# A two-block fp32 kernel on one core: TensorE multiplies a constant identity first, and the first k-tile's passes are put in another order

## The reference

```python
def hybrid_layer(x, norm_g, w_in, b_forget, pool_w, pool_scale, w_up_pool, w_up_attn, w_out):
    h = rmsnorm(x, norm_g)                        # 528 tokens (16 meta + 512) x 1024
    proj = jnp.einsum('bld,dn->bln', h, w_in)     # w_in: 1024 x 5128
    u_pool, z_pool, q, k, v, z_attn, f_logit, g_pool, g_attn = jnp.split(proj, _split_points(), axis=-1)
...
def reference(...):
    x = first_block(x, meta_tokens, norm_g, w_in, b_forget, pool_w, pool_scale, w_up_pool, w_up_attn, w_out,
                    final_norm_g)
    return second_block(x, c_2, g_norm1_2, w_in_2, g_q_2, g_k_2, rel_bias_2, w_o_2, g_norm2_2, w1_2, w2_2,
                        w_ada_2, b_ada_2)
```

## Time and profile before

| | |
|---|---|
| time, median of 3 runs | 1047.46 us (1045.13 to 1049.05) |
| the profiled execution's own time | 1048.44 us |
| its span, first to last instruction | 1046.4 us |
| TensorE matmuls busy | 992.7 us (95%) |
| TensorE weight loads busy | 817.5 us (78%) |
| VectorE busy | 675.7 us (65%) |
| ScalarE busy | 488.3 us (47%) |
| GpSimd busy | 86.1 us (8%) |
| mean granted TensorE clock | 0.988 |

### The profile page before, as it was taken

The page is one execution under the profiler, slowest core; times in us unless marked ns, Lnnn a source line. Parts: engine busy times, 40 slices in busy tenths (PEclk is TensorE's granted clock), DMA queues, the critical chain, the costliest instruction groups (busy, mean ns, idle before and its releaser), DMA issues.

```text
span 1046.4 us, 13120 instructions
## 1 busy us (share of the span) xinstructions
PE 992.7 (95%) x4760; PEld 817.5 (78%) x4760; DVE 675.7 (65%) x1270; ACT 488.3 (47%) x977; POOL 86.1 (8%) x195
## 2 busy tenths in 40 slices
PE   6998998999999999999998978889999999999998
PEld 4887887878888888766777756788878888888886
DVE  6386776785888759367678885778354445444453
ACT  6256776563232346477886764334224323412420
POOL 0000000110122011000003332001000000000000
PEclk9999999999999999998999998999999999999999
DMA  8133233128887523433213221525732322331211
GB/s 296 60 102 111 83 102 89 45 65 339 300 304 281 198 114 148 105 109 99 91 48 115 61 61 66 215 81 129 133 112 90 121 81 81 121 121 57 105 61 60
DMA packets 29535, 129.82 MB, mean 124 GB/s; under 512 B 3864, under 2 KB 3864, under 8 KB 19872
## 3 DMA queue, kind: packets, MB, share of 16 engines
q1 hardware_dynamic: 19984, 98.27, 29.0%
q0 software_dynamic: 7472, 26.75, 7.2%
q10 hardware_dynamic: 2016, 3.97, 1.1%
HBM read 118.40 MB, written 4.22 MB: 117 GB/s over the span
## 4 chain that ended last, share of the span: by engine, by line
PE 71%; DVE 15%; issue 5%; ACT 4%; DMA 4%; POOL 1%; SPq 0%; ACTq 0%; POOLq 0%; DVEq 0%
PE psum L1730 22%; PE psum L1731 21%; PE psum L1732 21%; DVE sgt L1192 2%; DVE wl L994 2%; DVE ptl L1209 2%; PE psum L1861 2%; PE psum L1840 1%; PE psum L1881 1%; DMA k_sb<-k_sb 1%; PE psum L1883 1%; DVE p_sb L1200 1%; DVE two L1531 1%; DMA x1b<-x_kept 1%; PE psum L2112 1%
## 5 line engine op out<-in xcount | busy, mean ns | idle before, releaser
L1730 PE MATMUL psum<-hh,wh 128*128 128x512 f32 (+1 forms) x720 | 277.3, 385 | 0.0
L1731 PE MATMUL psum<-hl,wh 128*128 128x512 f32 (+1 forms) x720 | 268.4, 373 | 0.0
L1732 PE MATMUL psum<-hh,wl 128*128 128x512 f32 (+1 forms) x720 | 268.2, 373 | 0.0
L519 ACT ACTIVATE wh<-raw 128x512 fp32r<-128x512 f32 x292 | 169.4, 620 | 134.2 <-PE psum L1732 119.9
L994 DVE TENSOR_TENSOR wl<-raw,wh 128x512 fp32r<-128x512 f32 x292 | 192.4, 684 | 18.0 <-ACT wh L519 17.7
L1732 PEld LDWEIGHTS psum<-hh,wl 128*128 128x128 f32 x720 | 136.0, 189 | 23.8
L1730 PEld LDWEIGHTS psum<-hh,wh 128*128 128x128 f32 x720 | 136.2, 189 | 22.9 <-issue 3.0
L1731 PEld LDWEIGHTS psum<-hl,wh 128*128 128x128 f32 x720 | 136.3, 189 | 18.6 <-issue 0.5
L1730 PE MATMUL psum<-wh,ah 128*128 128x512 f32 x320 | 127.6, 399 | 5.7 <-DVE wl L994 3.4
L1732 PE MATMUL psum<-wh,al 128*128 128x512 f32 x320 | 126.0, 394 | 0.0
L1731 PE MATMUL psum<-wl,ah 128*128 128x512 f32 x320 | 126.0, 394 | 0.0
(11 more groups left out here) (247 smaller groups left out, 1512.0 us busy)
## 6 DMA issues: line engine op xcount, KB each, us to landing
raw<-in_wall SPq DMA_DIRECT2D x75, 1024.0 KB, 4.9
wa<-in_wada POOLq DMA_DIRECT2D x20, 512.0 KB, 5.6
gt<-in_wada POOLq DMA_DIRECT2D x20, 512.0 KB, 6.1
wb<-in_wada POOLq DMA_DIRECT2D x8, 512.0 KB, 6.0
xt<-in_xcols SPq DMA_DIRECT2D x8, 264.0 KB, 8.4
cb<-c_rows SPq DMA_DIRECT2D x8, 264.0 KB, 3.3
x<-in_x SPq DMA_DIRECT2D x4, 512.0 KB, 8.3
x_kept<-x SPq DMA_DIRECT2D x4, 512.0 KB, 2.8
```

Source lines behind the costliest of these rows:

```text
L519: e.activation(home(w)[0][:, 512 * c:512 * c + 512], raw_of(w, c), ACT.Copy).then_inc(a["wh"], 1)
L1730: e.matmul(out_, lh, rh, start=start, stop=False, skip_group_check=True)
L1731: e.matmul(out_, lh, rl, start=False, stop=False, skip_group_check=True)
L1732: return e.matmul(out_, ll, rh, start=False, stop=stop, skip_group_check=True)
```

## The change

Only PE's program changes. Ahead of everything it multiplies `ident` with `ident` twelve times into bank 6, after the wait for the constants; nothing reads the result, and bank 6 is written afresh later. Then k-tile 0 is written out: five passes hh·wh after waits on `act_wh` and `act_hh0`, then five passes hh·wl after `dve_wl`, then five passes hl·wh after `dve_hl0`. K-tiles 1 to 3 are as they were.

```diff
             e.wait_ge(g["const"], 8)
             cuts = [(META + 128 * i, 128, bank[i]) for i in range(4)] + [(0, META, bank[7][0:META, :])]
-            for k in range(4):
+
+            for _ in range(12):
+                e.matmul(bank[6][:, 0:128], ident[:, :], ident[:, :], start=True, stop=True)
+
+            e.wait_ge(a["wh"], 1)
+            e.wait_ge(a["hh0"], 1)
+            for c0, rows, bk in cuts:
+                e.matmul(bk, hh[:, 0, c0:c0 + rows], wh[:, 0, 0:512], start=True, stop=False,
+                         skip_group_check=True)
+            e.wait_ge(v["wl"], 1)
+            for c0, rows, bk in cuts:
+                e.matmul(bk, hh[:, 0, c0:c0 + rows], wl[:, 0, 0:512], start=False, stop=False,
+                         skip_group_check=True)
+            e.wait_ge(v["hl0"], 1)
+            for c0, rows, bk in cuts:
+                e.matmul(bk, hl[:, 0, c0:c0 + rows], wh[:, 0, 0:512], start=False, stop=False,
+                         skip_group_check=True)
+            for k in range(1, 4):
                 e.wait_ge(v["wl"], k + 1)
                 e.wait_ge(v["hl0"], k + 1)
                 for c0, rows, bk in cuts:
-                    ins = by_rows(0, k, k, bk, (hh, hl), c0, rows, k == 0, False)
+                    ins = by_rows(0, k, k, bk, (hh, hl), c0, rows, False, False)
             ins.then_inc(t["half"], 1)
```

## The result

The changed kernel takes 1040.16 us (median of 6 runs, 1036.23 to 1040.8), against 1047.03 us before (6 runs, 1045.13 to 1050.6). The ratio is 0.9923, 95% interval 0.9907 to 0.994: 0.77% faster. That is 6.9 us where 3.0 to 3.6 were forecast, and outside the range of 1041.2 to 1047.6.

The account below looks back on a forecast made before the run. TensorE, 71% of the chain, was taken as the bound, first waiting 8.5 us for hl. Identity work and reordered passes gain 3.6 us in the profiled execution, 3.0 typically: 1047.46 to 1044.4 us, range 1041.2 to 1047.6.

Parts of the forecast that it names:

- The identity's cost: At TensorE's start: 24 records at half clock, 0.23 us each, 5.5 us in all, ending at 7.97 us.
- the rise: At TensorE's start: identity work begun at 2.45 us brings full clock between 5.8 and 8.5 us.
- The second k-tile: K-tile 1 on TensorE starts at 11.3 us against 14.87, 3.6 us earlier, bounds 3.2 and 3.7.
- DVE's row at 28.00: DVE's first 128x4 row behind TensorE comes at 28.1 us where it was 31.70.
- The two new waits on DVE: In k-tile 0, the waits for wl and hl before the later pass groups hold nothing.
- the middle of executions: Whole kernel: with a clock rise midway between 3.3 and 6.1 us, the gain is 3.0 us.
- I find nothing that takes the 3.6 us back: After the start: later operands and loads don't hold TensorE, so the whole chain keeps the 3.6 us.
- the first step of the part by part: At TensorE's start: twelve identity matmuls make 24 records from 2.45 us, costing 5.5 us, upper bound 6.5.
- C: Rival, 0.20: later half-speed clock stretches come out otherwise; one more cancels the gain, one or two fewer double it.
- B: Rival, 0.15: the identity lifts the clock late or not at all at the start; gain 0.8 to 1.8 us.
- D: Rival, 0.05: the identity runs at weight-load speed without lifting the clock; k-tile 1 starts 1.7 us late, 1049.2 us.

Follow-up runs that it names:

- e3: The kernel before with only the twelve identity matmuls added, k-tile 0 in the old order: 1041.91 us, ratio 0.9944.
- e4: The kernel before with twelve tiny 16 x 2 matmuls on the identity ahead of everything, 48 added records with hardly any work: 1043.75 us, ratio 0.9968.
- e6: The kernel before, with POOL issuing the four wb loads only after the last of the four x1b reloads has landed: 1043.44 us, ratio 0.9964.
- e7: The changed kernel with POOL's wb loads held until the x1b reloads have landed: 1040.47 us, ratio 0.9935.
- e5: The kernel before with 64 tiny 16 x 2 matmuls on the identity ahead of everything, 256 added records: 1047.63 us, ratio 1.0009.
- e1: The kernel before, unchanged, run and traced once more: 1048.12 us, ratio 1.0008.
- e2: The changed kernel without the identity matmuls, leaving only the new pass order of the first k-tile: 1047.73 us, ratio 0.9993.
- e8: The changed kernel with 8 identity matmuls in place of 12: 1041.54 us, ratio 0.9955.

## Why the prediction was wrong

**The start, right.** The identity's cost was right: the first 16 of its records took 3.57 us at half clock (the 17th starts at 5.93), 0.22 each where 0.23 was forecast. It was hidden, ending before the tokens came, and it was followed by the clock at full; the rise fell at 6.15 (records 0.21 us apart before, 0.11 after), inside the forecast 5.8 to 8.5. The Trainium skill ("TensorE: Matmul & The Clock Gate", "Part 1: The HAM clock gate") has it that activity releases the throttle, and by that rule products of an identity should release it too; the traces agree, as e3 and the changed kernel ran nothing else before the tokens and began these at full speed. The second k-tile started at 11.19 (11.3 forecast), and DVE's row at 28.00 (28.1). The two new waits on DVE held nothing.

**What the start is worth in the time, about right.** Against e4, which has the fetch moved and the old start, the changed kernel's median is 3.6 us lower (1043.75 to 1040.16), but from other sets of runs; each against its own kernel before, it is 6.9 - 4.1 = 2.8. Against e6 on the same chip, e7 is 3.0 lower (1043.44 to 1040.47), both with the loads in order. The identity alone is 1.8 lower than e4 (e3, the same chip). I gave 3.0 for the middle of executions and 3.6 for the profiled one. Single parts below 2 us can't be told apart with intervals of 2 us on either side; how the 3 us divide into clock and order stays open.

**The step that failed.** It is the sentence "I find nothing that takes the 3.6 us back", with the first step of the part by part: the twelve matmuls were costed as time alone, "24 records" of TensorE hidden in a wait. I asked only whether the gain would be lost later, and not what the records do as program. With their weight loads they are 48 instructions more ahead of everything, which should move each fetch of TensorE's program by 48 of 256. At the fetch by the reload TensorE had started 6318 records in the kernel before and 6324 in the changed one, 48 of them new: it came 42 records earlier in the old program. In e5 it came at 6574 = 6318 + 256, the old place. What the runs showed in its place: 4.1 us (e4, the records without the work), 4.2 us (e6, the loads ordered by hand), and nothing once the records made a whole piece (e5). The sum had no term for this. That the fetch fell away from the reload and not onto one was luck: nothing in the change aimed at it. 3.0 to 3.6 and 4.1 make 7.1 to 7.7; 6.9 was measured.

**The rivals.** The prediction gave times below 1042.2 a chance of 0.10, most of it to C, but by another mechanism, half-speed stretches that fall otherwise by chance. They did move: in the changed kernel two early ones take some 2 us from the lead, and it is back to 3.2 us by 500 us and to 4.0 by 640. But the mean clock is 0.988 in both executions, and what decided doesn't vary by chance. In the four traces with the fetch at the reload and the old loads (before, e1, e2, e5) the second gated addition comes 4.8 to 5.2 us after the first, TensorE waits 2.5 to 2.8 us, and a half-speed stretch of 3.4 us follows; in the other six the addition comes after 1.3 to 1.7 us, with no such wait and no such stretch. B and D are out by the profile: the clock was up and the identity ended in time.

**What stays open.** Why a fetch slows SP's issue isn't known. What is shown: in five traces with a fetch 0.10 to 0.22 us before the second issue (before, e1, e2, e5, e6), it took 1.26 to 1.65 us, in five without (after, e3, e4, e7, e8) 0.43. And the issue's end goes with the packet's: the packet took 1.05 us in the kernel before and 1.36 to 1.45 us in the other four, and in all five the issue ended 0.36 to 0.37 us after it. The same shows at another place, SP's loads of `sgt` (L485): there six of the ten traces have an issue of 1.06 to 2.21 us that ends 0.36 to 0.38 us after a packet. So the slow issue is tied closely to the packet, and e4, which moves the packets and hardly anything else, has it at 0.43. But not every issue beside a packet is held: in the kernel before, SP's issue at 288.26 lies within one and took 0.33 us, and at the reload itself the packet began during the first issue, at 650.94, which took 0.33 us too. What tells the issues that are held from those that aren't is open.

## What to carry to other kernels

Where TensorE waits at the start for its first operands, work on constants costs nothing as long as it ends before they come, and real work can then begin at full clock; order the passes by when their operands are ready, so that the wait is the shortest one. Before a small edit is credited with what it does, run a control that adds as many instructions without the work: here more than half of the gain came from the length of the program, and a gain of this kind goes again with the next edit that shifts it back, as in e5. And where two queues issue loads at once of which one is urgent, tie the other behind it by a semaphore, since a delay of one microsecond in one issue can turn their order round.

## What the runs showed of the hardware

TensorE's program arrives in 16 KB packets, one per 256 of its instructions on average (38 packets; 39 in e5, with 256 records more), and the page counts their time within the same 16 DMA engines as the data's. At the reload an issue on SP beside such a packet took 1.26 to 1.65 us in place of 0.43 and ended 0.36 to 0.37 us after the packet, while other issues beside a packet took their usual 0.33. With an issue of 1.26 us the second tile landed 8.9 us after it, behind two loads of the other queue, and with one of 0.43 us it landed after 4.7, ahead of them. Where plain work on the tokens came first, the clock rose 2.9 us (e1) to 6.1 us (before) after the first matmul of the same kernel. And after 3.4 us of identity work and 1.8 us of standing still the tokens' matmuls started at full speed (e8).
